# A hybrid decoder step on one core: cache copies leave the compression for the first norms and the routing units

## The chip, the cores and the metric

The kernel runs on one core of a Trainium2 chip. The metric is the device time of one execution in microseconds (us). The runs of the kernel before took 1332.22, 1333.13 and 1334.04 us, median 1333.13.

The engines are PE (TensorE, matrix products), DVE (VectorE), ACT (ScalarE), POOL (GpSimd) and SP (SyncE, which here only starts DMAs). Each engine runs its own list of instructions in order, and the lists meet in semaphores: an instruction adds to one when it has finished, and a `wait_ge` holds the rest of its engine's list until the count is there. A DMA is started by one of SP, ACT and POOL, and adds 16 to its semaphore when it has landed.

## What is computed

One decoder layer for a prompt of 256 rows and eight samples of eight new rows, width 1024. Cut to what matters:

```python
h = x @ w_in                                   # one projection, split into heads
o_A = dilated attention of 8 heads             # prompt, and samples against cache_a_k, cache_a_v
kc = gelu((rows + pe) @ w1) @ w2               # compression: windows of 32 cached rows, stride 16
o_B = gates * (compressed, selected, window attention)
x = layer_norm(ALPHA * x + concat(o_A, o_B) @ w_o)
q = x @ peer_wq; top 16 of keys twice, top 16 of pairs     # routing to 128*128 experts
y = sum over experts of gate * gelu(u . x) * v
x = layer_norm(ALPHA * x + y)
a_k_s = concat(cache_a_k, new)[:, 8:]          # updated caches, the same for a_v, win_k, win_v
```

The last line asks for the old caches again, shifted by the eight new rows. That is a plain copy of 37.4 MB from memory to memory. The kernel cuts it into 80 pieces, ten for each of the eight samples.

## The kernel before

There are five stages, each in a block of its own that ends when all engines have ended it: the projection (0 to 93 us), the compression with the attention of the prompt (93 to 285), the attention of the samples (285 to 406), output product, first norms and routing (406 to 570), and the experts (570 to the end).

**The compression** (`compress_block`) has eight units (`CMP_U`), each two samples' pages of keys or of values, and each unit four steps `j`. For a step ACT rounds the page rows to fp32r (`rows_hi`, line 186), DVE forms the rest (`split_pages_lo`, line 193), and PE does 24 of the unit's 96 products (`hidden`, line 605) in two PSUM banks `ph[h]`. After step 3 come the gelu of each bank on ACT (`gelu`, line 763) and, on PE, the small second product. The next unit's first product into a bank waits for the gelu of that bank. For units 0 and 1 the gelu waits for a bias that DVE copies out of the same bank (line 995). Between the steps lies one slice of the prompt's attention (`prompt`), whose steps end before step `CHOICE`, which is 26 of 32 (unit 6, step 2). From there on the block scores of the samples are computed (one exp on ACT, line 822). ACT loads a table when it changes between exp and gelu.

SP loads the pages of unit `u` (`load_cmp_pages`, line 412, 16 loads of 64 KB) when DVE has finished the splits of unit `u - 2`, since there are two buffers. ACT's first rounding of unit `u` stands in step 1 of unit `u - 1` and waits for all 16. Behind the compression's pages SP loads the selected pages of samples 0, 2 and 1 (`load_sel_pages`, line 397), window values, and keys and values of the first samples.

POOL makes the diagonal queries (`q_diag`, line 560) and in units 0 to 5 starts two cache copies in each step (`keep_copy`, line 390): copies 32 to 79.

**The routing** (`route_block`). PE forms the output product of three row tiles, DVE, ACT and POOL share each layer norm (POOL has the right columns, `norm.right`, lines 1404 and 1406), PE turns the normed rows (line 1544) and forms the query products (line 1549) with weights from a ring of four (`wq_ring`, line 1512), then the scores. Ten units follow, in each of which DVE finds the top 16 of four score rows, POOL adds the pairs (`pair_vals`, lines 1644 and 1645), DVE finds the top 16 of the pairs (`best_vals`) and makes a one-hot (`best_onehot`), POOL multiplies it with the pair ids (`onehot_ids`, line 1663), and DVE sums that in the next unit. After the product of units 0 to 7 POOL starts four copies, 0 to 31. PE forms some of the experts' hidden products in advance (`early`, line 1427), whose weights SP loads through a ring of four.

**The experts** (`expert_block`) need the ids. POOL gathers rows for the samples there, in its own DMA queue, behind any copies that are still in it. The copies must have landed only ahead of POOL's last norm part.

## Time and profile before

The profiled execution took 1332.8 us. Its span, from the first instruction to the last, is 1331.0 us.

| | before |
|---|---|
| median of three runs | 1333.13 us |
| profiled execution, its own time | 1332.8 us |
| its span | 1331.0 us |
| PE, DVE, ACT, POOL busy | 96%, 73%, 43%, 22% |
| mean DMA rate | 270 GB/s |
| mean granted clock of TensorE | 0.987 |

Busy shares are means over stages with different limits. A row of a timeline gives the start of an instruction, its length, the engine and the line, what it writes and reads, and in brackets how long the engine stood idle before it and what released it. [...] q0 is the DMA queue of POOL, q1 that of SP and q10 that of ACT.

### The profile page before, as it was taken

The numbers are of one execution on the slowest core, as the hardware profiler recorded it, in microseconds if no ns is written. First come the engines' busy times: TensorE is split into PE (matmuls) and PEld (weight loads), VectorE is DVE, ScalarE is ACT, GpSimd is POOL, SyncE is SP. The second block draws the span as 40 slices with busy tenths as digits, with TensorE's granted clock in tenths as the row PEclk, the third lists the DMA queues.
The fourth block names the chain that finished last, engine by engine and source line by source line (L and its number), as shares of the span: only waits on it lengthen the run. The fifth ranks groups of instructions, "written<-read, shape, count | busy, mean of one in ns | idle before, by whom it ended". The sixth has DMA issues, their size and how long they took to land.

```text
span 1331.0 us, 25923 instructions
## 1 busy us (share of the span) xinstructions
PE 1271.3 (96%) x8435; PEld 1081.4 (81%) x8436; DVE 974.2 (73%) x2220; ACT 573.7 (43%) x1058; POOL 294.5 (22%) x521
## 2 busy tenths in 40 slices
PE   9998599989899999999999999999999999999996
PEld 6888588866554777889998889889889888988985
DVE  4664366546634399989988887887888788888886
ACT  4643366534421211124345454454455444444453
POOL 0004132040001288711121111111122112212101
PEclk9998799999999999999999999999999999999998
DMA  8756577788974487859939999989988999998962
GB/s 289 225 160 190 167 248 243 261 276 325 403 303 167 144 285 287 290 199 260 287 122 330 318 311 315 319 312 312 321 309 308 323 312 309 322 317 301 324 196 92
DMA packets 164384, 358.79 MB, mean 270 GB/s; under 512 B 49235, under 2 KB 99091, under 8 KB 160595
## 3 DMA queue, kind: packets, MB, share of 16 engines
q1 hardware_dynamic: 134562, 242.51, 53.8%
q0 software_dynamic: 25424, 111.37, 23.9%
q10 hardware_dynamic: 4320, 3.93, 0.9%
q8 instruction: 41, 0.67, 0.2%
q14 instruction: 37, 0.30, 0.1%
HBM read 341.56 MB, written 53.35 MB: 297 GB/s over the span
## 4 chain that ended last, share of the span: by engine, by line
PE 50%; DVE 4%; issue 2%; DVEq 1%; ACT 1%; POOLq 0%; POOL 0%; ACTq 0%
PE psum L1918 25%; PE psum L1907 7%; PE psum L1906 7%; PE psum L1905 7%; PE psum L1427 2%; PE psum L1931 2%; DVE gated_i L2066 2%; DVE v_lo L2079 0%; DVEq L2066 0%; ACT v_hi L1987 0%; DVE OT L2062 0%; DVE ln_bn L1354 0%; DVE x L1348 0%; DVE gated_lo L2115 0%; DVE x L1377 0%
## 5 line engine op out<-in xcount | busy, mean ns | idle before, releaser
L1907 PE MATMUL psum<-x_hi,u_lo 128*128 128x256 f32 x760 | 215.1, 283 | 0.0
L1906 PE MATMUL psum<-x_lo,u_hi 128*128 128x256 f32 x760 | 215.0, 283 | 0.0
L1905 PE MATMUL psum<-x_hi,u_hi 128*128 128x256 f32 x760 | 214.6, 282 | 0.0
L2079 DVE TENSOR_TENSOR v_lo<-big,v_hi 128x1024 fp32r<-128x1024 f32 x128 | 156.7, 1224 | 35.1 <-ACT v_hi L1987 33.8
L1987 ACT ACTIVATE v_hi<-big 128x1024 fp32r<-128x1024 f32 x128 | 135.3, 1057 | 83.1 <-PE psum L1918 80.9
L1918 PE MATMUL psum<-v_hi,gated_hi 128*128 128x512 f32 x512 | 159.9, 393 | 1.1 <-DVE gated_lo L2115 1.0
L1918 PE MATMUL psum<-v_lo,gated_hi 128*128 128x512 f32 x512 | 158.7, 390 | 0.0
L1918 PE MATMUL psum<-v_hi,gated_lo 128*128 128x512 f32 x512 | 158.3, 390 | 0.0
L1906 PEld LDWEIGHTS psum<-x_lo,u_hi 128*128 128x128 f32 x760 | 145.5, 191 | 3.7
L1905 PEld LDWEIGHTS psum<-x_hi,u_hi 128*128 128x128 f32 x760 | 145.5, 191 | 3.7
L1907 PEld LDWEIGHTS psum<-x_hi,u_lo 128*128 128x128 f32 x760 | 145.5, 191 | 0.0
L2165 POOL DMA_INDIRECT gathered<-in_peer_v,v_rows_of x64 | 66.9, 1045 | 246.5 <-DVE OT L2098 225.4
L2075 DVE TENSOR_TENSOR u_lo<-big,u_hi 128x1024 fp32r<-128x1024 f32 x96 | 117.1, 1220 | 0.0
L1918 PEld LDWEIGHTS psum<-v_lo,gated_hi 128*128 128x128 f32 x512 | 96.1, 188 | 21.0
L1918 PEld LDWEIGHTS psum<-v_hi,gated_lo 128*128 128x128 f32 x512 | 96.1, 188 | 20.7
L2161 POOL DMA_INDIRECT gathered<-in_peer_u_rows,u_rows_of x64 | 62.6, 979 | 221.2 <-DVE sample_h L2071 217.8
L1918 PEld LDWEIGHTS psum<-v_hi,gated_hi 128*128 128x128 f32 x512 | 90.0, 189 | 15.7 <-DVE gated_lo L2115 1.6
L1996 ACT ACTIVATE big<-psum 128x256 f32<-128x256 f32 x96 | 36.2, 377 | 150.4 <-PE psum L1907 148.6
L1982 ACT ACTIVATE u_hi<-big 128x1024 fp32r<-128x1024 f32 x96 | 100.4, 1047 | 0.0
L605 PE MATMUL psum<-page_rows_hi,w_hi 128*128 128x256 f32 (+1 forms) x256 | 79.2, 309 | 10.9 <-ACT cmp_hidden L763 10.4
L2098 DVE SCALAR_TENSOR_TENSOR OT<-gathered,sample_h,OT 128x1024 f32<-128x1024 f32 x64 | 81.8, 1279 | 0.0
L265 PE MATMUL psum<-w_in_split,x_hi 128*128 128x512 f32 (+1 forms) x288 | 77.3, 376 | 2.6 <-DVE w_in_split L328 2.6
(323 smaller groups left out, 2518.8 us busy)
## 6 DMA issues: line engine op xcount, KB each, us to landing
big<-in_peer_v SPq DMA_DIRECT2D x128, 512.0 KB
big<-in_peer_u SPq DMA_DIRECT2D x115, 512.0 KB, 5.1
w_then_a_vals<-in_a_v SPq DMA_DIRECT2D x8, 2048.0 KB
keep_ak<-in_a_k POOLq DMA_DIRECT2D x32, 508.0 KB, 6.3
keep_av<-in_a_v POOLq DMA_DIRECT2D x24, 512.0 KB, 7.4
big<-in_a_k SPq DMA_DIRECT2D x4, 2048.0 KB, 13.3
a_keys<-in_a_k SPq DMA_DIRECT2D x4, 2048.0 KB, 12.4
wq_ring<-in_peer_wq SPq DMA_DIRECT2D x16, 512.0 KB, 5.6
```

The lines of the kernel that those rows point to most:

```text
L265: mm = pe.matmul(out[:, 0:c], a[:, P * i:P * i + P], b[:, u % 2, k * c:(k + 1) * c], start=(x + k + y == 0), stop=(x == 3 and k == 1 and y ...
L605: mm = pe.matmul(ph[h][:, 0:N], w[:, a, r, f, h * P:(h + 1) * P], x[:, r, S + f:S + f + N], start=(r == 0 and f == 0 and y == 0), stop=(r ...
L1905: pe.matmul(H[:, 0:SEQ], uh[:, q, kc], x1h[:, k, :], start=(k == 0), stop=False)
L1906: pe.matmul(H[:, 0:SEQ], uh[:, q, kc], x1l[:, k, :], start=False, stop=False)
L1907: mm = pe.matmul(H[:, 0:SEQ], ul[:, q, kc], x1h[:, k, :], start=False, stop=(k == KD - 1))
L1918: mm = pe.matmul(bank(2 * i + h), a[:, q, r], b[:, q, 512 * h:512 * (h + 1)], start=False, stop=stop and x == 2, skip_group_check=True)
L1982: act.activation(uh[:, q], us[:, q], ACT.Copy).then_inc(s["u_hi"], 1)
L1987: act.activation(vh[:, q], vs[:, q], ACT.Copy).then_inc(s["v_hi"], 1)
L2075: ve.tensor_tensor(ul[:, q], us[:, q], uh[:, q].bitcast(F32), ALU.subtract).then_inc(s["u_lo"], 1)
L2079: ve.tensor_tensor(vl[:, q], vs[:, q], vh[:, q].bitcast(F32), ALU.subtract).then_inc(s["v_lo"], 1)
L2098: ve.scalar_tensor_tensor(acc, gr[:, x], hs[:, bass.ds(m, 1)], acc, ALU.mult, ALU.add).then_inc(s["values"], 1)
L2165: gp.indirect_dma_start(gr[:, m % UN, :], None, d.peer_v.rearrange("a p n -> (a p) n"), bass.IndirectOffsetOnAxis(t.vix[:, m:m + 1], 0))\
```

## The change

Five things change.

1. No cache copy runs in the compression. Eight are started by POOL before its part of each of the three first norms (copies 48 to 71), eight after the third (72 to 79), and six instead of four in each of the routing units 0 to 7 (copies 0 to 47).
2. The selected pages of sample 2 are loaded by ACT, two in each of four steps from `CHOICE` on, and no longer by SP.
3. ACT does a gelu of one column ahead of the two gelus of each unit.
4. DVE does the page splits of unit 0 together at the start, where they were spread over three steps.
5. DVE does the arithmetic of the gates after the bias copy of unit 0, where it came before it.

```diff
-def load_sel_pages(eng, t, d, s, b):
+def load_sel_pages(eng, t, d, s, b, places=range(PAGES)):
-    for p in range(PAGES):
+    for p in places:
...
@@ compress_block, sync
             sp.dma_start(t.ka[1], d.a_k[1]).then_inc(s["ld_ka1"], 16)
-            load_sel_pages(sp, t, d, s, 2)
             sp.wait_ge(s["pages_lo"], 4 * NUC)
             load_sel_pages(sp, t, d, s, 1)
@@ gpsimd
                 for j in range(4):
-                    for x in range(2 if u < 6 else 0):
-                        keep_copy(gp, d, s, 32 + 8 * u + 2 * j + x)
@@ scalar
+            act.activation(warm[:], t.c0[:, 0:2], ACT.Copy).then_inc(s["warm"], 1)
+            act.wait_ge(s["warm"], 1)
...
                     if j == 3:
+                        act.activation(warm[:, 1:2], warm[:, 0:1], ACT.Gelu_apprx_tanh)
                         for h in range(2):
                             gelu(u, h)
...
                     prompt(u, j)
+                    if 4 * u + j >= CHOICE and 4 * u + j < CHOICE + 4:
+                        if 4 * u + j == CHOICE:
+                            act.wait_ge(s["p_scores"], NU)
+                        load_sel_pages(act, t, d, s, 2, range(2 * (4 * u + j - CHOICE), 2 * (4 * u + j - CHOICE) + 2))
@@ vector
                     if u == 0:
                         if j == 0:
-                            split_pages_lo(ve, t, s, 0, 1)
+                            for y in range(1, 4):
+                                split_pages_lo(ve, t, s, 0, y)
...
-                        if j < 2:
-                            split_pages_lo(ve, t, s, 0, 2 + j)
...
-                        if j == 3:
-                            gates()
...
                             ve.tensor_copy(bias[:, u, h:h + 1], ph[h][:, c:c + 1]).then_inc(s["cmp_bias"], 1)
+                    if (u, j) == (0, 3):
+                        gates()
@@ route_block, gpsimd
             gp.wait_ge(s["ld_xr"], 80)
             for i in range(TILES):
+                for x in range(8):
+                    keep_copy(gp, d, s, 48 + 8 * i + x)
                 norm.right(gp, i)
+            for x in range(24, 32):
+                keep_copy(gp, d, s, 48 + x)
...
                 if u < 8:
-                    for x in range(4):
-                        keep_copy(gp, d, s, 4 * u + x)
+                    for x in range(6):
+                        keep_copy(gp, d, s, 6 * u + x)
```

## Rows read from the trace of the kernel before

**Rows 1.** Busy by stage: PE, PEld, DVE, ACT, POOL; clock, DMA share, GB/s.

```profile
116.00:143.00 27.00, 16.08 (x110) 15.34 (x110) 3.47 (x13) 6.46 (x16) 10.92 (x26) 0.75 0.95 307
143.00:160.00 17.00, 11.89 (x65) 10.99 (x66) 9.56 (x37) 8.78 (x26) 1.53 (x4) 0.70 0.31 94
...
285.00:406.00 121.00, 108.19 (x1312) 67.77 (x1311) 66.77 (x144) 49.14 (x129) 1.54 (x4) 0.99 0.84 328
...
416.00:458.00 42.00, 40.29 (x196) 26.68 (x195) 19.10 (x61) 10.45 (x20) 6.30 (x6) 1.00 0.32 114
458.00:566.00 108.00, 104.39 (x481) 82.32 (x479) 102.63 (x498) 16.83 (x36) 85.48 (x233) 1.00 0.82 290
```

**Rows 2.** Timelines of PE and ACT: start, length, instruction, idle before and releaser.

```profile
117.65 0.58 PE L605 MATMUL psum<-page_rows_hi,w_hi 128*128 128x290 f32 x1 [3.71 <-ACT cmp_hidden L763]
...
143.59 0.69 PE L671 MATMUL psum<-p_turned,h_keep 128*64 128x128 f32 x4 [9.86 <-ACT OT L754]
...
154.30 0.55 PE L605 MATMUL psum<-page_rows_hi,w_hi 128*128 128x256 f32 x1 [4.52 <-ACT cmp_hidden L763]
142.37 0.63 ACT L186 ACTIVATE page_rows_hi<-sel_pages 128x512 fp32r<-128x512 f32 x1 [15.29 <-DMA sel_pages<-in_cmp_pool]
```

**Rows 3.** DMA queues from 128 to 142 us: packets, MB, share of 16 engines.

```profile
q0 software_dynamic: 509, 4.47, 96.5%
q1 hardware_dynamic: 529, 0.24, 6.9%
```

**Rows 4.** The page loads, line 412, from 150 to 179 us.

```profile
L412 SPq DMA_DIRECT2D sel_pages<-in_cmp_pool x16: 333/333/341, 159.2 to 175.5; - x16
...
DMA to landing us min/median/max: 1.7/3.6/7.0
```

**Rows 5.** Timeline of SP's queue: the page loads of units 2 and 3.

```profile
105.04 44.33 SPq L412 DMA_DIRECT2D sel_pages<-in_cmp_pool  x32
```

**Rows 6.** Timelines of DVE and ACT: the bias copy and the table load, unit 0.

```profile
115.49 0.20 DVE L995 COPY cmp_bias<-psum 128x1 f32<-128x1 f32 x2
115.71 1.28 ACT L763 ACT_TABLE_LOAD   x1 [2.71 <-DVE cmp_bias L995]
```

**Rows 7.** The products of line 605 from 118 to 122 us: PE, PEld, clock, DMA.

```profile
118.00:122.00 4.00, 4.00 (x18) 4.00 (x18) 0.50 1.06 387
```

**Rows 8.** Timeline of PE: the first product of unit 7.

```profile
266.60 0.35 PE L605 MATMUL psum<-page_rows_hi,w_hi 128*128 128x256 f32 x1 [2.19 <-ACT cmp_hidden L763]
```

**Rows 9.** The issue of a copy, line 390: ns min/median/max, first and last start.

```profile
L390 POOL DMA_DIRECT2D keep_ak<-in_a_k x32: 523/532/747, 116.2 to 544.5; - x32
```

**Rows 10.** Timelines of DVE and POOL at the first norms.

```profile
416.42 1.28 DVE L1348 SCALAR_TENSOR_TENSOR x<-x_rows,psum 128x512 f32<-128x512 f32 x2 [17.09 <-DMA ln<-in_ln_b]
421.29 1.00 POOL L1404 TENSOR_TENSOR x<-x,ln 128x384 f32<-128x384 f32 x1 [134.75 <-ACT x L1397]
...
426.68 1.00 POOL L1404 TENSOR_TENSOR x<-x,ln 128x384 f32<-128x384 f32 x1 [3.31 <-ACT x L1397]
```

**Rows 11.** Timelines of POOL and DVE, one round of a routing unit.

```profile
539.80 3.20 POOL L1663 TENSOR_TENSOR onehot_ids<-best_onehot,pair_ids 128x1600 f32<-128x1600 bf16 x1 [1.76 <-issue]
...
545.01 1.36 POOL L1644 TENSOR_TENSOR pair_vals<-top_vals 128x32 f32<-128x32 f32 x8
546.33 0.20 POOL L1645 TENSOR_TENSOR pair_vals<-top_vals 128x16 f32<-128x16 f32 x1
...
550.02 3.20 POOL L1663 TENSOR_TENSOR onehot_ids<-best_onehot,pair_ids 128x1600 f32<-128x1600 bf16 x1 [1.61 <-issue]
546.63 0.31 DVE L1690 MAX8 best_vals<-pair_vals 128x8 f32<-128x50 f32 x2
```

**Rows 12.** DMA queue of POOL's copies from 458 to 566 us.

```profile
q0 software_dynamic: 1792, 15.08, 37.6%
```

**Rows 13.** The loads of the query weights, line 1512: issue to landing.

```profile
DMA to landing us min/median/max: 3.5/5.6/12.3
```

**Rows 14.** Timeline of PE: the turn of the expert ids.

```profile
565.98 0.30 PE L1592 MATMUL psum<-c,expert_ids 128*128 128x128 f32 x1 [0.24 <-DVE expert_ids L1705]
```

More of the change, by code:

```diff
@@ L465, in compress_block @@
         bias = sb("cmp_bias", [P, 2, 2])
+        warm = sb("gelu_warm", [P, 2])
         pp, pT, qd = t.pp, t.pT, t.qd
@@ L2273 @@
         "keep_wk": (NB, P, 512 - NT), "keep_wv": (NB, P - 2, 4 * P)}
-FRONT_SEMS = """x_in0 x_in1 x_in2 x_in3 w_hi w_lo w_used h_low proj w_in0 w_in1 w_in2 c0 w1k w1v w1_hi w1_lo w2 idle own_hi own_lo pages_hi pages_lo rows_used cmp_first evac roped out0 out_kv gate gate_e gate_a
+FRONT_SEMS = """x_in0 x_in1 x_in2 x_in3 w_hi w_lo w_used h_low proj w_in0 w_in1 w_in2 c0 w1k w1v w1_hi w1_lo w2 idle warm own_hi own_lo pages_hi pages_lo rows_used cmp_first evac roped out0 out_kv gate gate_e gate_a
 turned turned_out turned_act rope_c cmp_pg0 cmp_pg1 cmp_bias cmp_turn cmp_hid cmp_gelu cmp_second cmp_done""".split()
```

## The prediction

> **What bounds the kernel now.** An average over the span (PE is 96% busy) says nothing about where a copy hurts, so I cut the span into stages first [rows 1]. Read each row for the engine that is nearly full, and for the clock. In the compression (93 to 285 us) PE works only 16.08 of 27 us from 116 to 143 and 11.89 of 17 from 143 to 160, at a mean granted clock of 0.75 and 0.70, with the DMA engines at 95% and then 31%. In the sample attention (285 to 406) the DMA engines are 84% busy. In the routing (458 to 566) DVE is busy for 102.63 of 108 us. So the compression has a hole, and the routing has none.
>
> Next come the timelines of ACT and PE across the hole [rows 2]. ACT stands for 15.29 us until 142.37, waiting for the pages of unit 2, and PE stands 9.86 us behind it. On either side PE waits for a gelu, 3.71 us until 117.65 and 4.52 us until 154.30. The DMA queues say why the pages are late [rows 3]: from 128 to 142 the software queue, which carries POOL's copies, held 96.5% of the DMA engines and moved 4.47 MB in 509 packets, while SP's queue, with the pages, moved 529 packets but only 0.24 MB. With fewer copies beside them the 16 pages of a later unit are issued in 16.3 us and land 3.6 us after their issue at the median [rows 4]. Unit 2's were begun at 105.04 [rows 5]: 16.3 and a landing end by 125, before ACT's wait began at 127.1. So the copies make this wait, and SP's issue rate does not.
>
> **What the compression gives back.** All 48 copies leave it.
>
> (a) PE's stall of 9.86 us goes. The splits drawn forward on DVE let SP begin unit 2's pages sooner, which adds room but is not needed. Late next is ACT itself.
>
> (b) The gelu waits. In unit 0 ACT waited 2.71 us for the bias copy, which ran at 115.49 behind the four small operations of the gates, and then a table load of 1.28 us stood before the gelu [rows 6]. The diff puts the gates behind the bias, which saves between 0 and 2.71 us (I take 1.2, four operations of 0.3), and the warm-up gelu lets the table load run while ACT would wait: 1.2 + 1.28, so 2.4 of the 3.71 us go. In the 4.52 us ACT and DVE catch up after the page wait, since all were released at 142.4 together, and a table load lies in it too. I take all of it. Together 6.9 us. Where ACT is not idle ahead of the gelu the warm-up moves nothing.
>
> (c) The clock. [...] By the row at 0.50 and the starts at 143.59 and 154.30 some 14 us of work ran slow, so I take 6.9 us. The drops followed waits of 3.7 to 10 us, and the one that is left would be 1.3 us. (a) to (c): 23.7 us.
>
> (d) The pages can become the next limit: 16.3 + 3.6 us of issue and landing against units of PE that take some 18 to 21 us without the stall. Bounds 0 to 8 us over four units; I take 1, since each unit's pages are begun more than one unit ahead of their use.
>
> (e) ACT issues the eight page loads of buffer 2, two to a step. SP takes 16.3 / 16 = 1.0 us for one [rows 4], and so, I take, does ACT. The first two stand between the last exp and the gelu of unit 6, for which PE already waits 2.19 us [rows 8]: +2.0 us, bounds 0 to 3. The warm-up does not help there, since the exp needs its own table until then. The other six lie beside PE's work. SP's next load gets 8 us sooner, but its last one waits for the end of the compression anyway. The sample attention keeps its DMA limit and its prefetches and only starts earlier.
>
> Compression: 23.7 - 1 - 2 = 20.7 us less, bounds 15 to 25.
>
> **The 32 copies around the first norms.** One issue holds POOL for 532 ns, at most 747 [rows 9], eight for 4.2 us. DVE is released by the `ln` load at 416.42 and POOL with it, so the first eight end at 420.6, before ACT lets POOL's part of norm 0 begin at 421.29 [rows 10]: the wait for ACT hides them, and if it were gone they would cost 4.2 us. That part takes 2.1 us; the second eight then end at 427.6, where the part of norm 1 began at 426.68. It is 0.9 us late, and PE's turn and the query products queue behind it. The third eight make norm 2 some 0.7 us late, where PE has queries of two steps to do first. The last eight run in POOL's idle time before the first routing unit. +0.9 us, bounds 0 to 2.
>
> [...]
>
> **Two more copies in each of eight routing units.** The loop through POOL and DVE has no slack [rows 11]. POOL's product begins at 539.80 and, four copies and the next `pair_vals` later, again at 550.02: 10.22 us. In between `pair_vals` ends at 546.53 and DVE begins `best_vals` at 546.63, only 0.1 us after it. DVE's `best_onehot`, which that leads to, is what POOL's product waits for. So POOL's way round and DVE's are equally long today. Two more copies add 1.06 us to POOL's, of which 0.1 to 0.2 are slack: 0.87 x 8 = +6.9 us, and POOL becomes the bound of these units. Bounds: 0 if an issue overlaps with POOL's product, 8.5 with no slack.
>
> **Contention.** In the routing the software queue moved 15.08 MB in 37.6% of 108 us, 40.6 us, so 371 GB/s [rows 12]. That is the 32 copies that run there already, 0.47 MB each, so the 48 that come are 22.5 MB and want 61 us. Free are (1 - 0.32) x 42 = 28.6 us before 458 and (1 - 0.82) x 108 = 19.4 after it [rows 1], with the 8 us of slip 56: the stage becomes saturated, with some 5 us left over for the stage behind it. The query weights have landed in 3.5 to 12.3 us [rows 13] with four in flight. PE's early products end only 0.24 us before the ids are there [rows 14], but now have 7.8 us more. Bounds 0 to 8; I take +2, nearer to none, because DVE and not a load ends these units.
>
> **Sum.** The profiled execution took 1332.8 us with a span of 1331.0; the median of the runs is 1333.13, 0.3 us above it, so one may stand for the other. 1332.8 - 20.7 + 0.9 + 6.9 + 2 = **1322 us**. The gate matrix and the expert loop are not touched.
>
> **The rivals.**
> - Cover in the routing: POOL's issues overlap with its arithmetic, and the 6.9 us do not come. 1315 us. Against it, the rows of POOL follow one another without overlap [rows 11]. Chance 0.12.
> - The pages next: 19.9 us of issue and landing set the pace of four units, 8 us instead of 1. 1329 us. For it, units of 18 to 21 us. 0.14.
> - Slower: the query weights starve as the pages did. If SP's queue had only 6.9% until the 15 MB of the norm copies are through, 40 us after 417, the weights of the second query step, needed at about 434, would be there at 457. The scores slip by 23 us: 1322 - 2 + 23 = 1343. It decides from a slip of 13 us on. Against it, in [rows 3] both queues moved as many packets, and only the size differed: 8.8 KB a packet against 0.45. The weights have rows of 4 KB, which by that gives them 0.3 of the rate, 110 GB/s, and the four in flight land by 440. 0.09. [...]
> - POOL's issues are held by DVE. With one of DVE's operations of 0.7 us ahead of each of 16 copies, the norms end 11 us later: 1333. Against it, the 747 ns. 0.03.
> - The change does not do what it says: the pages are late though the copies are gone, and only 2.4 us of gelu wait go. 1332.8 - 2.4 + 9.8 = 1340. 0.03.
>
> **How the numbers follow.** The forecast has 0.59, with a range of its own of 1317 to 1327 from the clock term and the contention. With the first two rivals it is 0.85, and the range is 1314 to 1331. A measurement of this kernel can tell about 0.2%, 2.7 us, from no change. Faster: 0.83, the forecast (0.58), cover (0.12) and most of the pages (0.13). Same: 0.06, POOL held and the ends of two others. Slower: 0.11, the starving queries, no effect, and less than 0.01 of the rest.
>
> **What would show it.** Right: no wait of ACT for the compression's pages above 2 us; PE over 95% busy from 116 to 250 at a clock of 1.00; unit 2 starting near 134 instead of 154.30; the compression ending 20 us earlier; PE's wait for unit 6's gelu grown to 4 us; POOL's product every 11.1 us instead of 10.2 in the routing, with DVE waiting for `pair_vals`. Wrong: a wait for query weights or early products of more than 5 us, a clock drop that stays, or a gate matrix stage that grows because its gathers stand behind copies in POOL's queue.

## The result and the profile after

The changed kernel takes **1336.4 us** (median of 16 runs, 1334.6 to 1342.4) against 1332.6 us (median of 16) for the kernel before beside it. The ratio is 1.0033, with an interval of 1.0023 to 1.0043: it is slower by 0.33%. The forecast was 1322 us, faster than before, with a range of 1314 to 1331, and the time lies outside it. Its profiled execution took 1335.9 us with a span of 1334.1, 3.1 us more than the span before.

Read the stages first. Busy time by stage of the changed kernel: PE, PEld, DVE, ACT, POOL; then clock (the mean granted clock of TensorE, as a share of full speed), DMA share, GB/s (the profile's shares of a full stretch come out a little above 1 in places, here up to 1.04).

```profile
116.00:143.00 27.00, 26.33 (x223) 24.21 (x222) 16.14 (x60) 14.83 (x45) 4.07 (x14) 1.00 0.21 58
143.00:160.00 17.00, 17.00 (x146) 14.57 (x145) 10.01 (x38) 11.05 (x35) 2.36 (x8) 1.00 0.20 55
160.00:250.00 90.00, 85.69 (x703) 75.01 (x704) 51.61 (x150) 52.17 (x146) 12.78 (x32) 0.98 0.41 136
434.00:455.00 21.00, 20.16 (x88) 14.39 (x86) 18.07 (x84) 5.33 (x8) 13.03 (x27) 1.00 1.01 381
455.00:469.00 14.00, 1.08 (x5) 0.69 (x4) 12.82 (x55) 0.60 (x1) 12.16 (x37) 0.63 1.04 405
540.00:553.00 13.00, 7.01 (x34) 5.87 (x32) 11.87 (x64) 0.77 (x2) 9.45 (x38) 0.91 1.00 377
```

The hole of [rows 1] is filled: PE works 26.33 of 27 and 17.00 of 17 us at a clock of 1.00, and the first product of the sample attention starts at 265.43 us instead of 285. But two new holes stand in the routing. From 455 to 469 PE works 1.08 of 14 us while the DMA engines are full, and from 540 to 553 it works 7.01 of 13, again beside full DMA engines.

The timeline of PE in the changed kernel says what each hole waits for. The columns are those of [rows 2].

```profile
387.07 17.55 PE L1538 MATMUL psum<-big,OT 128*128 128x512 f32 x48 [0.90 <-PEq L1014]
...
434.68 13.09 PE L1554 MATMUL psum<-x1T,wq_ring 128*128 128x320 f32 x48
...
468.15 19.48 PE L1554 MATMUL psum<-x1T,wq_ring 128*128 128x320 f32 x64 [12.92 <-DMA wq_ring<-in_peer_wq]
488.16 1.16 PE L1583 MATMUL psum<-peer_keys,peer_q 128*128 128x128 f32 x8 [0.53 <-ACT peer_q L1616]
...
552.98 16.30 PE L1432 MATMUL psum<-x1T,big 128*128 128x256 f32 x64 [5.99 <-ACT early_hidden L1442]
569.12 0.27 PE L1597 MATMUL psum<-c,expert_ids 128*128 128x128 f32 x1
```

The output product starts 19.05 us earlier (387.07, before 406.12), and that is all the compression gives. **The first debt** is the query weights: the third group of query products waits 12.92 us for them. The second group, which the slower rival of the prediction had in view, starts at 434.68 with no wait. **The second debt** comes at 552.98, 5.99 us behind ACT (in the kernel before PE's last wait of this kind was 1.79 us). The ids are turned at 569.12, where they were turned at 565.98 before [rows 14]: 3.1 us late, and the span is 3.1 us longer.

What stands in front of the weights is seen in the timeline of SP's queue and in the DMA queues from 428 to 469 us of the changed kernel (packets, MB, share of 16 engines; then the issues, KB each, median us to landing).

```profile
439.18 1.81 SPq L1424 DMA_DIRECT2D big<-in_peer_u  x4
441.04 46.95 SPq L1517 DMA_DIRECT2D wq_ring<-in_peer_wq  x8
```

```profile
q0 software_dynamic: 1115, 9.81, 63.2%
q1 hardware_dynamic: 1568, 5.71, 36.8%
...
wq_ring<-in_peer_wq SPq DMA_DIRECT2D x6, 512.0 KB, 26.6
```

SP's queue moved 5.71 MB in 41 us, 139 GB/s, the rest went to copies. A block of query weights, 0.52 MB, takes 3.8 us at that rate, less than PE's 4.35 us for its products (17.39 / 4). So the weights alone would keep up. But the four loads of early products' weights (`load_early`, 2.1 MB, 15 us at 139 GB/s) stand ahead of block 8, and block 8 is what PE waits for: it is issued at 441.04 and lands 27.1 us later, at 468.1.

The second debt in the timeline of ACT, changed kernel:

```profile
539.28 0.34 ACTq L1445 DMA_DIRECT2D early_hidden_of<-early_hidden  x1
...
552.45 0.38 ACT L1442 ACTIVATE early_hidden<-psum 128x256 f32<-128x256 f32 x1 [11.95 <-DMA early_hidden_of<-early_hidden]
...
564.49 0.47 ACT L1630 ACTIVATE best_vals<-best_vals 128x320 f32<-128x320 f32 x1
```

ACT copies an early product out of PSUM and stores it to memory, from two buffers. The store issued at 539.28 frees its buffer only at 552.45. ACT stands 11.95 us for it, PE behind ACT, and the gates' exp, which comes later in ACT's list, runs only at 564.49. The waits of the changed kernel from 385 to 572 us say who paid (us in total, times, longest):

```profile
ACT early_hidden L1442 <- DMA early_hidden_of<-early_hidden: 21.5, 4, 11.9
...
DVE gate_sum L1745 <- ACT best_vals L1630: 9.4, 1, 9.4
...
DVE best_vals L1699 <- POOL pair_vals L1654: 6.7, 7, 1.8
```

DVE had finished its units and stood 9.4 us for that exp.

**The ledger.** It goes first by POOL's products of the routing units. Timeline of POOL, kernel before (units 0 and 9) and changed kernel (units 0, 3, 4 and 9):

```profile
463.63 3.21 POOL L1663 TENSOR_TENSOR onehot_ids<-best_onehot,pair_ids 128x1600 f32<-128x1600 bf16 x1 [1.56 <-DVE best_onehot L1728]
560.24 3.54 POOL L1663 TENSOR_TENSOR onehot_ids<-best_onehot,pair_ids 128x1600 f32<-128x1600 bf16 x1 [1.79 <-issue]
```

```profile
445.30 3.21 POOL L1672 TENSOR_TENSOR onehot_ids<-best_onehot,pair_ids 128x1600 f32<-128x1600 bf16 x1 [1.55 <-DVE best_onehot L1737]
483.40 3.20 POOL L1672 TENSOR_TENSOR onehot_ids<-best_onehot,pair_ids 128x1600 f32<-128x1600 bf16 x1 [1.55 <-issue]
500.42 3.20 POOL L1672 TENSOR_TENSOR onehot_ids<-best_onehot,pair_ids 128x1600 f32<-128x1600 bf16 x1 [1.76 <-issue]
555.11 3.54 POOL L1672 TENSOR_TENSOR onehot_ids<-best_onehot,pair_ids 128x1600 f32<-128x1600 bf16 x1 [1.77 <-issue]
```

POOL's product of unit 0 runs 18.3 us earlier than before, so the norms cost 19.05 - 18.3 = 0.7. From there to the product of unit 9 13.2 us go. In seven rounds the loss is 0.83 to 0.97 us each, 6.4 in all; the eighth, from unit 3 to 4, takes 17.02 us instead of 10.21, which is 0.9 more for the copies and 5.9 for the weights. From POOL's last product to the turn of the ids the changed kernel takes 14.0 us and the one before 5.7, 8.3 us more. Sum: -19.05 + 0.7 + 7.3 + 5.9 + 8.3 = +3.15, and the ids come 3.14 us later.

The 8.3 us are not the stores' alone. The turn of the ids stands in PE's list behind the early products, so the list has to be read too. Timeline of PE, kernel before: the first early product, and the last wait for ACT.

```profile
492.06 3.62 PE L1427 MATMUL psum<-x1T,big 128*128 128x256 f32 x16
555.14 10.60 PE L1427 MATMUL psum<-x1T,big 128*128 128x256 f32 x48 [1.79 <-ACT early_hidden L1437]
```

In the changed kernel PE comes to its first early product at 489.15. Of the 19.05 us only 2.9 are left there: 12.92 went to the wait for weights and 2.1 to the slower products behind it (19.48 us for 64 of them, 17.39 before, at a mean clock of 0.89 from 468 to 488 us), the rest to the norms. From there to the turn of the ids PE takes 80.0 us, before 73.9, so 6.05 more, of which 4.2 are the longer last wait for ACT. An estimate from these numbers: with the old 73.9 us PE would have turned the ids at 563.1, where POOL's and DVE's way would have had them at 555.11 + 5.74 = 560.9. So of the 8.3 us some 2.2 are the late weights again, by PE's way, and some 6 the stores. Together that is about 8 us for the weights and 6 for the stores. Such shares depend on which is counted first, because the two ways run side by side: taken away alone, the late weights give back 12 us (`e2_early_later` below) and the stores 5.5 (`e8_three_buffers`).

### The profile page after: what moved, and what is told of

Its sections match the earlier page's. It is cut to its first block, busy times and chain, and to the rows that moved or that the text cites. A ratio compares the mean times of both kernels' runs of the same rounds, so it can differ in the third digit from the quotient of the medians.

```text
span 1334.1 us, 25942 instructions
## 1 busy us (share of the span) xinstructions
PE 1272.1 (95%) x8436; PEld 1080.0 (81%) x8436; DVE 975.3 (73%) x2220; ACT 575.6 (43%) x1067; POOL 308.1 (23%) x521
## 4 chain that ended last, share of the span: by engine, by line
PE 50%; DVE 4%; issue 2%; DVEq 1%; ACT 1%; POOLq 0%; POOL 0%; ACTq 0%
PE psum L1927 25%; PE psum L1916 7%; PE psum L1915 7%; PE psum L1914 7%; PE psum L1432 2%; PE psum L1940 2%; DVE gated_i L2075 2%; DVE v_lo L2088 0%; DVEq L2075 0%; ACT v_hi L1996 0%; DVE OT L2071 0%; DVE ln_bn L1359 0%; DVE x L1353 0%; DVE gated_lo L2124 0%; DVE x L1382 0%
## 5 line engine op out<-in xcount | busy, mean ns | idle before, releaser
L2174 POOL DMA_INDIRECT gathered<-in_peer_v,v_rows_of x64 | 78.8, 1231 | 234.8 <-DVE OT L2107 213.7
L1927 PEld LDWEIGHTS psum<-v_hi,gated_lo 128*128 128x128 f32 x512 | 96.1, 188 | 20.7
L1554 PE MATMUL psum<-x1T,wq_ring 128*128 128x320 f32 (+2 forms) x288 | 74.2, 418 | 14.4 <-DMA wq_ring<-in_peer_wq 13.2
```

The source lines that it names most:

```text
L1554: mm = pe.matmul(bank(j % 2)[:, c], wq[:, j % 4, k, :], xT[:, k, c], start=(k == 0), stop=(k == KD - 1))
L1927: mm = pe.matmul(bank(2 * i + h), a[:, q, r], b[:, q, 512 * h:512 * (h + 1)], start=False, stop=stop and x == 2, skip_group_check=True)
L2174: gp.indirect_dma_start(gr[:, m % UN, :], None, d.peer_v.rearrange("a p n -> (a p) n"), bass.IndirectOffsetOnAxis(t.vix[:, m:m + 1], 0))\
```

## The experiments

Runs in which copies are left out say so, and their last wait for the copies counts that many fewer, which the excerpts below do not show; every other run computes everything. The numbers are medians, with the lowest and highest run behind them.

### Which copies make which wait

`e1_no_norm_copies` leaves out copies 48 to 79:

```diff
             for i in range(TILES):
-                for x in range(8):
-                    keep_copy(gp, d, s, 48 + 8 * i + x)
                 norm.right(gp, i)
-            for x in range(24, 32):
-                keep_copy(gp, d, s, 48 + x)
```

> The changed kernel without the 32 copies around the first norms (copies 48 to 79 are left out of the computation; six per routing unit stay). In its profile the first norms start 19.4 us earlier than before, the scores of routing unit 4 only 2.9 us earlier, and the ids come 3.1 us later. Theory A, two separate debts: the query weights wait (12.92 us of PE, which reaches POOL's round as 6.5 us) is made by the norm copies; the wait of ACT for an early product's store (11.9 us, 8.2 us on the path) is made by six copies in each unit. Then the wait for weights goes, the store wait stays: 1336.4 - 6.5 - 0.7 = 1329 us. Theory B, one debt: the store waits behind a backlog that the norm copies began, so both go: 1336.4 - 15 = 1321 us. Theory C (POOL's issue time is all of it, six copies a unit): no change, 1336 us.

Measured: **1324.5 us** (1320.8 to 1325.8). The wait for weights is gone, the waits for stores are not: 37.2 us of ACT's idle time are put down to them in seven pieces, and PE stands 8.2 us behind ACT. The time lies between the two theories. The late weights needed the norm copies, as A says, but taking these away gave 12 us and not 7. A had priced the weights by POOL's round (6.5 us); by PE's list they cost more. PE begins its early products 15 us sooner (474.4, not 489.2) and then takes 84.9 us to the turn of the ids instead of 80.0, so that they are turned at 559.3, 9.8 us sooner. The two debts aren't separate: both lie on PE's way to the ids.

`e3_four_per_unit` leaves out copies 32 to 47 instead:

```diff
                 if u < 8:
-                    for x in range(6):
-                        keep_copy(gp, d, s, 6 * u + x)
+                    for x in range(4):
+                        keep_copy(gp, d, s, 4 * u + x)
```

> The changed kernel with four instead of six copies in each of routing units 0 to 7 (copies 32 to 47 are left out of the computation; the 32 around the norms stay). POOL's round goes from 11.1 back to 10.2 us. Theory A (six per unit make the store wait): the store wait shrinks and with it the 8.2 us, POOL's 7.6 us come back too, the weights' 6.5 us stay; PE's early products, which then end about 561.5, set the end: 1336.4 - 7.6 = 1329 us. Rival D (the store wait is there in any case, as before had one of 7.75 us): PE's early products still end at 569, and POOL's faster round only waits: 1335 to 1337 us.

Measured: **1322.9 us** (1322.2 to 1324.2), 13.5 less. Theory A in kind, rival D falls, but A's size was 6 us short. PE waits 9.62 us for weights, POOL's round is 10.2 us again, and PE does 11 early products in one piece:

```profile
463.30 19.16 PE L1554 MATMUL psum<-x1T,wq_ring 128*128 128x320 f32 x64 [9.62 <-DMA wq_ring<-in_peer_wq]
...
517.38 38.25 PE L1432 MATMUL psum<-x1T,big 128*128 128x256 f32 x176
555.47 0.27 PE L1597 MATMUL psum<-c,expert_ids 128*128 128x128 f32 x1
```

The longest wait of ACT for a store is 5.1 us here and none reaches PE. So the stores' debt comes with six copies in a unit, and the weights' with the 32 of the norms.

`e4_neither` is both edits together, 48 copies left out:

> The changed kernel with neither: no copies around the norms and four per routing unit (48 of the 80 copies are left out of the computation). It is the compression without copies with the routing of before. The compression gives back 19.0 us, the routing is as before: 1332.6 - 19 = 1314 us. If it stays above 1320 us, something beside the copies (the loads that ACT starts, or DVE's order) costs in the later stages; if it comes below 1310, the copies cost the routing something before, too.

Measured: **1314.0 us** (1312.9 to 1314.6), as expected. It is the gain of the compression with the routing of before.

### Is it the copies, or what stands in front of the weights?

`e2_early_later` leaves every copy where the change puts it and moves four loads on SP:

```diff
             for j in range(HH):
                 if j >= 4:
                     sp.wait_ge(s["q_mm"], j - 3)
-                if j == 8:
+                if j == 12:
                     sp.wait_ge(s["o_mm"], TILES - 1)
                     for n in range(4):
                         load_early(sp, d, t, s, n)
```

> The changed kernel with one order changed on SP: the four loads of the early products (2.1 MB) are started behind query weights 8 to 11, not ahead of them. Theory A: SP's queue has about a third of the DMA engines in this stretch, 130 GB/s, by which a query weight block of 0.52 MB takes 4.0 us, as long as PE's step of 4.35; so it isn't the copies alone but the 2.1 MB ahead of weight block 8, 16 us at that rate, that makes the wait of 12.92 us. The wait falls below 3 us and unit 4 of the routing comes 6.5 us earlier: 1330 us. Rival: the weights starve beside the copies whatever stands ahead of them; the wait moves to weight blocks 8 to 11 or to the early products and stays above 8 us: 1335 to 1337 us.

Measured: **1324.3 us** (ten runs; ratio to before 0.9951, 0.9929 to 0.9974), 12 us less than the changed kernel, by one number in the code. Theory A holds and again gives more than its 6.5 us: PE begins its early products at 473.49 and turns the ids at 555.41, 13.7 us sooner. The timeline of PE at the place of the 12.92 us:

```profile
454.58 17.39 PE L1554 MATMUL psum<-x1T,wq_ring 128*128 128x320 f32 x64
472.50 1.16 PE L1583 MATMUL psum<-peer_keys,peer_q 128*128 128x128 f32 x8 [0.53 <-ACT peer_q L1616]
```

There is no wait at all, beside a DMA share of 1.02 from 458 to 490 us. So full DMA engines alone don't starve a load of 4 KB rows here; it takes 2.1 MB in front of it, in its own queue, as well. The stores are still held in this run: ACT waits 40.6 us for them in ten pieces, and PE 7.3 us for ACT. How the two queues shared the engines in the changed kernel is in the DMA rows of 428 to 469 us: 1568 packets of SP's queue beside 1115 of the copies', which are 2.4 times as large (8.8 KB against 3.6). So they shared neither packets nor bytes (5.71 MB beside 9.81) equally.

`e8_three_buffers` asks for the stores by themselves: it gives the early products' rows a third buffer.

```diff
+    h = n % 3
     act.wait_ge(s["hp_mm"], n + 1)
-    if n >= 2:
-        act.wait_ge(s[f"st_h{m}"], 16 * (n // 2))
-    act.activation(t.hp[:, m], t.psum[:, 5 + 2 * m, 0:SEQ], ACT.Copy).then_inc(s["hp_out"], 1)
+    if n >= 3:
+        act.wait_ge(s[f"st_h{h}"], 16 * (n // 3))
+    act.activation(t.hp[:, h], t.psum[:, 5 + 2 * m, 0:SEQ], ACT.Copy).then_inc(s["hp_out"], 1)
...
```

> The changed kernel with three buffers instead of two for the early products' hidden rows, so that ACT waits for the store of three products ago and not of two. Theory A (a store that takes 13 us to land beside six copies holds ACT, ACT holds PE, and that sets when the ids are there): PE's stall of 5.99 us shrinks by the time of one product, 3.5 us, with part of the clock drop behind it: 1331 to 1333 us against 1336.4. Rival E (the ids wait for something else, such as PE's late start after the query weights): no change, 1335 to 1337 us.

Measured: **1330.9 us** (1327.6 to 1334.4; ratio to before 0.9993, 0.9979 to 1.0007), 5.5 us less than the changed kernel. By the median that is theory A, and near the 6 us of the ledger. Its trace does not show this gain, for the profiled execution was the slowest of the ten (1334.4 us). In it PE turns the ids at 567.68, 1.4 us sooner than in the changed kernel, and by as much its wait for query weights is shorter (11.52 us, not 12.92). The wait behind ACT is gone, but PE waits about as long for the next thing in line, the early products' own weights:

```profile
PE psum L1432 <- DMA big<-in_peer_u: 6.3, 4, 4.1
```

### What the compression's gain is made of

`e7_copies_out_only` is the kernel before with its 48 copies of the compression left out and no other edit:

```diff
                 for j in range(4):
-                    for x in range(2 if u < 6 else 0):
-                        keep_copy(gp, d, s, 32 + 8 * u + 2 * j + x)
```

> The kernel before with only the 48 copies of the compression left out of the computation, and none of the other edits. Beside the run with neither (19.4 us less in the span) it gives the copies' own share. Theory A, as the prediction's terms: PE's stall of 9.86 us, the gelu wait behind it and the clock, 17 to 19 us in all: 1314 to 1316 us. Rival: the other edits carry 5 us or more of it, and the time is above 1318 us.

Measured: **1314.3 us** (1312.6 to 1318.7), theory A: within the spread of the runs the copies alone are the whole gain of `e4_neither`, 1314.0.

`e6_edits_only` is the changed kernel with all copies at their old places:

```diff
+                    for x in range(2 if u < 6 else 0):
+                        keep_copy(gp, d, s, 32 + 8 * u + 2 * j + x)
...
-                    for x in range(6):
-                        keep_copy(gp, d, s, 6 * u + x)
+                    for x in range(4):
+                        keep_copy(gp, d, s, 4 * u + x)
```

with the norms' copies taken out as in `e1_no_norm_copies`.

> The changed kernel with all 80 copies where they were before (two per step in compression units 0 to 5, none around the norms, four per routing unit): only the edits on ACT, DVE and SP are left. The prediction gave them 2.4 us of the gelu wait less 2.0 us for ACT's page loads. Theory A: the page wait stays, since the copies make it: 1330 to 1333 us. Rival: the page splits drawn forward let SP begin unit 2's pages ahead of the burst of copies, and the wait goes without moving a copy: 1313 to 1320 us.

Measured: **1323.1 us** (1322.6 to 1326.0), 8 us less than before with every copy in place. Neither theory: the page wait stays but shrinks from 15.29 [rows 2] to 8.91 us, until 131.25, and PE stands 3.48 us behind it instead of 9.86.

```profile
131.25 0.63 ACT L186 ACTIVATE page_rows_hi<-sel_pages 128x512 fp32r<-128x512 f32 x1 [8.91 <-DMA sel_pages<-in_cmp_pool]
```

Of the edits, `e13_splits_only` makes one in the kernel before:

```diff
                         if j == 0:
-                            split_pages_lo(ve, t, s, 0, 1)
+                            for y in range(1, 4):
+                                split_pages_lo(ve, t, s, 0, y)
                         turned_out(4 * j)
                         turned_out(4 * j + 2)
                         if j == 0:
                             evac_last(ve, t, s, len(WCOLS) - 1)
-                        if j < 2:
-                            split_pages_lo(ve, t, s, 0, 2 + j)
```

> The kernel before with one edit: DVE's three page splits of unit 0 that were spread over steps 0 and 1 stand together at the start. SP may then begin unit 2's pages at 101.7 us and not at 105.0. Theory A: most of the 8 us of e6_edits_only come from here, since the 3.4 us put eleven of 16 loads ahead of the first copy at 116 us, and unit 2's last page lands at 131 and not at 142: 1324 to 1327 us. Rival: the table load taken ahead (ACT) and the gates moved behind the bias give it: this run stays at 1330 to 1333 us.

Measured: **1320.9 us** (1319.1 to 1326.6). Theory A, and 3 us below its range: this edit alone gives what all of them give, within the spread of the two runs. SP's queue and ACT in this run:

```profile
101.53 46.20 SPq L412 DMA_DIRECT2D sel_pages<-in_cmp_pool  x32
```

```profile
130.57 0.63 ACT L186 ACTIVATE page_rows_hi<-sel_pages 128x512 fp32r<-128x512 f32 x1 [3.10 <-DMA sel_pages<-in_cmp_pool]
```

SP begins unit 2's pages 3.5 us sooner than at 105.04 [rows 5], and they are there 11.8 us sooner than at 142.37 [rows 2], because 13 of the 16 are started before the first copy at 116 us, where it was 10. ACT's wait is shorter than in `e6_edits_only` only because ACT comes to it 5 us later; the pages are there at nearly the same time (130.57 and 131.25), and unit 2 starts at 142.4 and 142.5. In front of unit 7, where `e6_edits_only` has ACT's page loads, PE waits 4.21 us there and 2.19 us here.

### A better place for the copies

`e5_paced` spreads them over four places, with the order of loads of `e2_early_later`:

```diff
@@ compression, gpsimd
+                    if u < 6:
+                        gp.wait_ge(s["pages_lo"], 4 * u + j + 1)
+                        keep_copy(gp, d, s, 32 + 4 * u + j)
@@ sample attention, gpsimd
+            for x in range(2):
+                gp.wait_ge(s[f"ld_wo{x}"], 32)
+            for x in range(12):
+                keep_copy(gp, d, s, 56 + x)
@@ norms (and four instead of six per routing unit)
+                for x in range(4):
+                    keep_copy(gp, d, s, 68 + 4 * i + x)
                 norm.right(gp, i)
```

> All 80 copies, placed by what the runs so far show: one copy in each step of compression units 0 to 5, each behind a wait for DVE's page splits of that step (24 copies), 12 in the sample attention behind the landing of the output weights (in the changed kernel no DMA runs from 372.5 to 387 us), four ahead of each first norm's right part (12), four per routing unit (32), and the early products' loads behind query weights 8 to 11. Theory A (a copy hurts by what waits beside it, bursts in front of small packets, a full queue beside weights and stores, a sixth issue on POOL): the compression keeps its 19.4 us and the routing is at 10.2 us a unit with no wait for weights: 1313 to 1316 us. Rival (any copy beside the page loads or the weights costs about its transfer, 1.3 us): 24 + 12 copies cost 20 us or more and the time is above 1325.

Measured: **1333.2 us** (1325.9 to 1336.1), 17 us above theory A. The timelines of POOL and PE show one reason:

```profile
379.91 1.95 POOL L390 DMA_DIRECT2D keep_av<-in_a_v  x4
```

```profile
397.09 19.67 PE L1545 MATMUL psum<-big,OT 128*128 128x512 f32 x48 [9.75 <-PEq L1017]
```

POOL's last issue ends at 381.9, but the next stage begins for all engines at 397, some 2 us after the last of these copies has moved (the copies' queue is at 82.2% from 385 to 397 us, and idle from about 395). By this run, and by the next, in which the 9.75 us go with the copies, the end of a stage waits for the transfers that POOL started in it. So an idle stretch of DMA at a stage's end was no free place here. This trace is of the fastest of the 13 executions, 7.3 us below their median, and does not show what the others lost. In it ACT waits only 2.3 us for pages, and the next run, with the same compression, waits 6.28; that the usual execution lost its time there is likely and not shown.

`e9_paced_24_24` has the twelve copies at the norms instead:

```diff
@@ against e5_paced: no copies in the sample attention, and
+                for x in range(4):
+                    keep_copy(gp, d, s, 56 + 4 * i + x)
                 norm.right(gp, i)
+            for x in range(12):
+                keep_copy(gp, d, s, 68 + x)
...
```

> As the run e5_paced, but without copies in the sample attention: 24 copies in the compression, each behind DVE's page splits of its step, 24 around the first norms (four ahead of each right part, 12 behind the third), four per routing unit (32), early products' loads behind query weights 8 to 11. All 80 copies run. [...] Theory A: a stage's end waits for POOL's own copies, and that is all of e5_paced's loss: 1325.9 - 9.75 - 2.1 = 1314 us, up to 1317 us. Rival (the paced copies in the compression are what made e5_paced slow and its times wide): 1325 to 1334 us again.

Measured: **1322.8 us** (1320.7 to 1324.6). The 9.75 us at the stage's end are gone (PE stands 0.90 us there), and so are the sum's 2.1 us, which are the output product's: its 48 products took 19.67 us in `e5_paced`, at a mean granted clock of 0.76 from 396 to 407 us, and take 17.56 here, at 1.00. But the sum misses by 6 us or more: ACT waits for unit 2's pages again.

```profile
128.34 0.63 ACT L186 ACTIVATE page_rows_hi<-sel_pages 128x512 fp32r<-128x512 f32 x1 [6.28 <-DMA sel_pages<-in_cmp_pool]
```

POOL comes to its first copies only at 116 us, when the waits of units 0 and 1 are met already, and starts eight by 125.7. The sample attention starts at 271.79 us, 6.4 us later than in the changed kernel (265.43).

`e10_burst_24_24` is `e9_paced_24_24` without the line `gp.wait_ge(s["pages_lo"], 4 * u + j + 1)`:

> As e9_paced_24_24, but the 24 copies of the compression are started as before, with no wait for DVE, four to a unit as POOL comes to them. Theory A (what hurts the page loads is how many copies are in the queue at once): the first eight are in flight at 116 us together, but 24 copies are half of before's and nothing is behind them: within 2 us of e9. Rival (the pace itself matters): PE waits again in unit 2, 3 us or more above e9.

Measured: **1322.3 us** (1322.2 to 1322.8), within 1 us of it, as theory A says. But it doesn't test the pace: the wait hardly moves the copies. The first eight are issued from 116.07 to 125.7, in `e9_paced_24_24` from 115.95 to 125.7.

`e11_paced_48` keeps all 48 copies in the compression, two to a step, and none at the norms (four per routing unit as in the others):

```diff
+                    if u < 6:
+                        gp.wait_ge(s["pages_lo"], 4 * u + j + 1)
+                        for x in range(2):
+                            keep_copy(gp, d, s, 32 + 8 * u + 2 * j + x)
```

> All 48 copies of the compression stay there, two in a step as before, but each step's pair waits for DVE's page splits of that step; none around the norms, four per routing unit, early products' loads behind query weights 8 to 11. Theory A (bursts, not bytes): at two copies, 2.5 us of transfer, in a step of some 5 us the page loads get through between them, and the compression costs at most 3 us more than e9's: 1314 to 1318 us. Rival (bytes: 48 copies beside the page loads of 512-byte rows are too many however they are spread): ACT waits for pages as in e6_edits_only, 1321 to 1325 us.

Measured: **1323.9 us** (1321.3 to 1325.3), the rival's number. But its reason, the bytes, doesn't hold: with twice the copies of `e9_paced_24_24` in the compression it is only 1 us slower, or about 2 if the 24 copies that the other has at the norms are priced as `e14_norms_only` prices them below. What all three runs share are the copies between 116 and 126 us, beside unit 2's page loads. That left the place, and `e12_units_2_to_5` leaves out only the start: 16 copies in units 2 to 5, 32 at the norms as in the changed kernel, four per routing unit, loads in the order of `e2_early_later`. All 80 run.

```diff
@@ compression, gpsimd
+                    if 2 <= u < 6:
+                        gp.wait_ge(s["pages_lo"], 4 * u + j + 1)
+                        keep_copy(gp, d, s, 24 + 4 * u + j)
```

> All 80 copies run: 16 in compression units 2 to 5, one a step behind DVE's page splits of that step, none in units 0 and 1; 32 around the first norms as in the changed kernel; four per routing unit (32); early products' loads behind query weights 8 to 11. In e9_paced_24_24 ten copies of units 0 and 1 ran together from 116 us and unit 2's pages came 6.28 us late; units 3 to 6 showed no wait for pages. Theory A: the place decides, only the loads begun at 102 us have no room; the compression keeps all its 19 us and the time is that of e14_norms_only within 1 us: 1313 to 1316 us. Rival: copies cost their bytes anywhere in the compression, 16 of them two thirds of e9's 7 us: 1318 to 1321 us.

Measured: **1314.1 us** (1313.1 to 1315.2; ratio to before 0.9859, 0.9842 to 0.9877). Theory A. Eight copies fewer than in `e9_paced_24_24`, and none before 133.7 us, give 8.7 us, where the bytes alone would have given a third of its loss. With all copies running it is as fast as the run that leaves 48 out, and it is 18.7 us under the kernel before of the same chip and 22 under the changed one (on another chip). Its stages, the same columns as above:

```profile
116.00:143.00 27.00, 26.34 (x223) 24.23 (x223) 15.86 (x60) 14.60 (x45) 5.60 (x17) 1.00 0.30 87
143.00:160.00 17.00, 17.00 (x146) 14.57 (x145) 10.15 (x39) 11.23 (x35) 3.48 (x11) 1.00 0.51 162
...
430.00:458.00 28.00, 26.66 (x116) 19.09 (x115) 21.74 (x102) 6.37 (x10) 16.31 (x44) 1.00 1.00 381
458.00:490.00 32.00, 31.47 (x148) 24.16 (x147) 31.04 (x160) 4.69 (x10) 25.32 (x73) 1.00 1.00 384
```

From 458 to 490 us the DMA engines are as full as in the changed kernel, and PE works 31.47 of 32 us.

`e14_norms_only` is that kernel without its 16 copies in the compression (left out), to price the norms' 32 by themselves:

> As e2_early_later, with four instead of six copies per routing unit (copies 32 to 47 are left out of the computation). It prices the 32 copies around the norms, beside the run with neither (1314.0 us). Theory A: with the weights in order they cost POOL's 0.7 us at norm 1 and little more, and e2's remaining 8 us are the sixth and fifth copy of each unit: 1314.5 to 1316 us. Rival: the backlog in the queue still holds weights or stores: 1318 us or more.

Measured: **1315.3 us** (1314.2 to 1316.5), theory A. Against `e4_neither` the 32 copies cost at most 1.3 us: the two ran on different chips, and the kernel before took 1332.7 us beside this run and 1331.9 beside that one. The 16 copies of `e12_units_2_to_5`, on the same chip, cost nothing that can be told (1314.1 with them, 1315.3 without).

## Why the prediction was wrong

**What bounds the kernel, and the compression: right.** -20.7 us forecast, -19.05 measured. Unit 2 starts at 134.43, and PE is 96% busy from 116 to 250 us, as listed (the clock is 1.00 until 160 and 0.98 behind it). The 6.9 us of the clock are an estimate from how long PE may have run slow, and no run shows this term by itself; what the traces show in its place is a clock of 1.00 from 116 to 160 us, where it was 0.75 and 0.70 [rows 1]. The stall of 9.86 us is gone and no wait for pages is left, so (d) is 0. Unit 0's gelu wait went from 3.71 to 1.11 us, 2.6 against 2.4. (e) is right in mechanism and size: PE's wait in front of unit 7 is 4.21 us, against 2.19 [rows 8] and a forecast of 2.0 more. `e7_copies_out_only` shows that the copies carry all of it. The sentence that the splits drawn forward add room that "is not needed" is true beside the moved copies, and hid the cheapest gain of the diff: alone they give 11.8 us.

**The norms: right.** +0.9 forecast, 0.7 in the trace, at most 1.3 as a run.

**Two more copies per unit: right.** A round of 11.05 to 11.2 us against 11.1, 7.3 us against 6.9, with DVE waiting for `pair_vals`.

**Contention: this is the step that failed.** It was given +2 with bounds 0 to 8 and measured 5.9 + 8.3 = 14.2 us. With 19.05, 0.7, 7.3 and 14.2 in their places the prediction's own sum gives 1336.0, so this step is the whole miss but for 2 us. The estimate of the rate was good: 110 GB/s for SP's queue, measured 139. The sentence that the four blocks in flight land by 440 was not so good: SP starts them one by one from 421.8 to 432.3, as the ring comes free, and they land from 434.3 to 448.0, just in time. And the step asked only when those four land, and not what SP starts next. The listing has it, 2.1 MB at `j == 8`, ahead of block 8, which PE needs at 455. The sum could have been made with the prediction's own rate, and `e2_early_later` shows that the order is what decides: blocks 4 to 7, the 2.1 MB and block 8 are 4.7 MB, 43 us at 110 GB/s, from 422 when the ring first comes free to 465, a wait of 10 us. The second half wasn't looked at: ACT's stores. The trace before held the warning, a row of ACT's timeline near the end of the routing:

```profile
554.61 0.38 ACT L1437 ACTIVATE early_hidden<-psum 128x256 f32<-128x256 f32 x1 [7.75 <-DMA early_hidden_of<-early_hidden]
```

The reason given for the small value, "DVE and not a load ends these units", looked at the units and not at PE's second way to the same end, which had 0.24 us of slack [rows 14].

**The rivals.** The slower one had the right kind of cause, and its chance of 0.09 was too small. Its place was wrong (the second group of weights, which came in time), and so was its size (23 us). It said that it decides from a slip of 13 us; the weights made 5.9 us at routing unit 4 and about 8 at the ids, and only with the stores, which it did not name, are there 14. The others fell: POOL's issues aren't hidden by its arithmetic, DVE doesn't hold them (one copy's issue around the norms takes 526 ns at the median and 901 at most), and the pages didn't become the limit.

## What to carry to other kernels

A transfer that is moved has to be priced against every queue at its new place, and for each queue by what is issued next and when that is needed, not by what is in flight; in `e2_early_later` DMA engines at a share of 1.02 made no query weight late, since the things wanted first stood first. Where two ways lead to one end, give the slack of both. And before moving a load away, ask whether the late one can be started earlier: three reordered splits gave 11.8 us in the kernel before, one reordered group of loads 12 in the changed one.

## What was not expected of the hardware

- Full DMA engines alone didn't delay PE: with a share of 1.00 from 430 to 490 us the query products of `e12_units_2_to_5` wait 0.28 us in all for weights.
- Beside page loads of 512-byte rows copies weigh far more: eight of them between 116 and 126 us made ACT wait 6.28 us in `e9_paced_24_24`, while the 16 of `e12_units_2_to_5`, begun from 133.7 us on, once unit 2's pages were through, cost nothing that can be told (1314.1 us with them, 1315.3 without). How much of that is the later pages' slack and how much that fewer copies are in flight at once isn't separated.
- The next stage began 15 us after POOL's last issue in `e5_paced`, when its copies had landed. SP's transfers did not hold a stage so: in the changed kernel a 2 MB load that SP started at 263.04 was still moving when the sample attention began at 265.43 (SP's queue moved 1.59 MB from 265 to 269 us). Which instruction holds the stage's end isn't seen in the trace.
- A store of 128 KB took 13.4 us to land at most in the changed kernel, with six copies in a unit, 9.5 at most before and 7.5 in `e3_four_per_unit`, both with four; its median changed little, 3.9 us before and 4.4 in both others. It is the tail that holds an engine.
